# A decoder layer in float32: the low part of every fourth gate/up weight unit made by an accumulating DMA in place of VectorE

## The reference

```
def swiglu(h, w_gate, w_up, w_down):
    return (jax.nn.silu(h @ w_gate) * (h @ w_up)) @ w_down
...
        h = rms_norm(x, norm_ffn[layer])
        x = x + swiglu(h, w_gate[layer], w_up[layer], w_down[layer])
    return rms_norm(x, norm_final)
```

## Time and profile before

| | |
|---|---|
| median of 3 runs | 1426.72 us (1426.65 to 1428.62) |
| span of the profiled execution, from first to last instruction | 1425.4 us |
| time of the profiled execution beside its span | none is given apart from it; the median of the runs is 1.3 us longer than the span |
| TensorE busy | 1413.8 us, 99% |
| DVE busy | 785.1 us, 55% |
| ACT busy | 650.4 us, 46% |
| POOL busy | 42.6 us, 3% |
| DMA, all queues | 260.10 MB, mean 182 GB/s |

### The profile page before, as it was taken

The page is one execution under the profiler, slowest core; times in us unless marked ns, Lnnn a source line. Parts: engine busy times, 40 slices in busy tenths (PEclk is TensorE's granted clock), DMA queues, the critical chain, the costliest instruction groups (busy, mean ns, idle before and its releaser), DMA issues.

```text
span 1425.4 us, 17803 instructions
## 1 busy us (share of the span) xinstructions
PE 1413.8 (99%) x6433; PEld 1155.3 (81%) x6433; DVE 785.1 (55%) x944; ACT 650.4 (46%) x810; POOL 42.6 (3%) x62
## 2 busy tenths in 40 slices
PE   9999999999999999999999999999999999999997
PEld 8999887777788888888888888888888878888886
DVE  6455567667655658655555454554555554544354
ACT  7433356656545654454543333434343333434343
POOL 4000000000000110000000000000000000000000
PEclk9999999999999999999999999999999999999999
DMA  7766665454565666555666666666666666555563
GB/s 243 202 188 187 195 216 168 133 147 135 150 190 162 190 200 210 177 179 182 183 184 181 188 181 186 178 188 185 184 179 188 183 197 196 187 192 188 172 206 118
DMA packets 138272, 260.10 MB, mean 182 GB/s; under 512 B 8448, under 2 KB 29504, under 8 KB 137840
## 3 DMA queue, kind: packets, MB, share of 16 engines
q1 hardware_dynamic: 137552, 256.08, 60.5%
q0 software_dynamic: 640, 3.37, 0.7%
q10 hardware_dynamic: 32, 0.01, 0.0%
HBM read 257.33 MB, written 2.10 MB: 182 GB/s over the span
## 4 chain that ended last, share of the span: by engine, by line
PE 99%; DMA 0%; ACT 0%; DVE 0%; issue 0%; SPq 0%; ACTq 0%; DVEq 0%
PE bank L566 31%; PE bank L568 31%; PE bank L567 31%; PE bank L553 2%; PE bank L709 1%; PE bank L631 0%; DMA x<-in_x 0%; PE bank L708 0%; PE bank L601 0%; PE bank L603 0%; PE bank L602 0%; PE bank L632 0%; PE bank L756 0%; PE bank L748 0%; PE bank L734 0%; PE bank L762 0%
## 5 line engine op out<-in xcount | busy, mean ns | idle before, releaser
L1096 DVE TENSOR_TENSOR weight_lo_ring<-raw_ring,weight_hi_ring 128x1024 fp32r<-128x1024 f32 (+2 forms) x488 | 594.4, 1221 | 547.9 <-ACT weight_hi_ring L911 375.6
L911 ACT ACTIVATE weight_hi_ring<-raw_ring 128x1024 fp32r<-128x1024 f32 (+1 forms) x284 | 295.6, 1042 | 456.8 <-PE bank L568 455.0
L566 PE MATMUL bank<-weight_hi_ring,hT_hi 128*128 128x512 f32 (+2 forms) x768 | 306.0, 398 | 0.0
L904 ACT ACTIVATE weight_hi_ring<-raw_ring 128x1024 fp32r<-128x1024 f32 (+2 forms) x204 | 213.2, 1050 | 200.9 <-PE bank L568 185.2
L568 PE MATMUL bank<-weight_hi_ring,hT_lo 128*128 128x512 f32 (+2 forms) x768 | 296.3, 386 | 0.0
L567 PE MATMUL bank<-weight_lo_ring,hT_hi 128*128 128x512 f32 (+2 forms) x768 | 296.2, 386 | 0.0
L566 PE MATMUL bank<-weight_hi_ring,h2T_hi 128*128 128x512 f32 x704 | 278.4, 395 | 0.0
L568 PE MATMUL bank<-weight_hi_ring,h2T_lo 128*128 128x512 f32 x704 | 277.5, 394 | 0.0
L567 PE MATMUL bank<-weight_lo_ring,h2T_hi 128*128 128x512 f32 x704 | 277.4, 394 | 0.0
L566 PEld LDWEIGHTS bank<-weight_hi_ring,hT_hi 128*128 128x128 f32 x768 | 144.8, 189 | 29.1 <-issue 3.6
L567 PEld LDWEIGHTS bank<-weight_lo_ring,hT_hi 128*128 128x128 f32 x768 | 144.9, 189 | 27.1 <-issue 2.6
(11 more groups left out here) (200 smaller groups left out, 759.5 us busy)
## 6 DMA issues: line engine op xcount, KB each, us to landing
raw_ring<-in_w_in SPq DMA_DIRECT2D x96, 512.0 KB, 3.6
raw_ring<-in_w_gate SPq DMA_DIRECT2D x88, 512.0 KB, 4.3
raw_ring<-in_w_up SPq DMA_DIRECT2D x88, 512.0 KB, 3.8
raw_ring<-in_w_down SPq DMA_DIRECT2D x88, 512.0 KB, 4.4
raw_ring<-in_w_in SPq DMA_DIRECT2D x56, 452.0 KB, 3.5
raw_ring<-in_w_out SPq DMA_DIRECT2D x32, 512.0 KB, 3.8
raw_ring<-in_w_br_c SPq DMA_DIRECT2D x16, 256.0 KB, 4.6
raw_ring<-in_w_br_a SPq DMA_DIRECT2D x16, 256.0 KB, 7.5
```

The costliest lines, as they stand in the source:

```text
L566: pe.matmul(dst, x_hi, w_hi, start=first and k == 0, stop=False)
L904: act.activation(whi[:, s, :, 0:width(u)], raw[:, s, :, 0:width(u)], ACT.Copy).then_inc(hi_ready, 1)
L911: act.activation(whi[:, s, :, 0:cols], raw[:, s, :, 0:cols], ACT.Copy).then_inc(hi_ready, 1)
L1096: dve.tensor_tensor(lo, w, hi.bitcast(F32), ALU.subtract).then_inc(lo_ready, 1)
```

## The change

In the hardware loop of gate and up (ten iterations), the units of slot 3, every fourth, get their low part in another way: ACT writes `-raw`, rounded to float32r, into `wlo` right after the high part, and a DMA issued by POOL adds `raw` onto it. That is 4 units an iteration, 40 in all (`A_UNITS`). DVE leaves them out. The DMA counts in `lo_added`, for which TensorE waits ahead of these units. Since the DMA reads `raw`, SP may load over slot 3 only when it is through; SP waits for `unit_used` of the unit there in place of `lo_ready`, in all 11 iterations and for the first units of slot 3 in the down stage. As DVE no longer counts every unit, `lo_ready` becomes four semaphores, one a slot.

```
+A_FIRST = U_FFN + 2 * UPC + LAG
+A_UNITS = (NC_F - 1) * 2 * UPC // RING
+
+
+def made(u):
+
+    return u // RING + 1 - (A_UNITS if u % RING == RING - 1 and u >= U_DOWN else 0)
...
-        lo_ready = sem("lo_ready")
+        lo_ready = [sem(f"lo_ready{i}") for i in range(RING)]
+        negated = sem("hi_negated")
+        lo_added = sem("lo_added_by_dma")
...
                     for j in range(UPC):
                         u0 = U_FFN + c * UPC + j
-                        sp.wait_ge(lo_ready, i * (2 * UPC) + (u0 - RING + 1))
+                        if u0 % RING == RING - 1:
+                            sp.wait_ge(unit_used, i * (2 * UPC) + (u0 - RING + 1))
+                        else:
+                            sp.wait_ge(lo_ready[u0 % RING], i * (2 * UPC // RING) + made(u0 - RING))
                         load(u0 % RING, w[:, UK * j:UK * j + UK, bass.ts(i, W)])
...
                         u0 = U_DOWN + c * UPD + j
-                        sp.wait_ge(lo_ready, i * (2 * UPD) + (u0 - RING + 1))
+                        if (c, j) == (0, RING - 1):
+                            sp.wait_ge(unit_used, i * (2 * UPD) + (u0 - RING + 1))
+                        else:
+                            sp.wait_ge(lo_ready[u0 % RING], i * (2 * UPD // RING) + made(u0 - RING))
...
+            for n in range(A_UNITS):
+                pool.wait_ge(negated, n + 1)
+                pool.dma_start(wlo[:, RING - 1, :, :], raw[:, RING - 1, :, :],
+                               accum_op=ALU.add).then_inc(lo_added, 16)
+
             pool.wait_ge(unit_used, U_DOWN)
...
                         u0 = U_FFN + c * UPC + j
-                        pe.wait_ge(lo_ready, i * (2 * UPC) + (u0 + 1))
+                        if u0 % RING == RING - 1:
+                            pe.wait_ge(lo_added, i * 64 + (16 * ((c * UPC + j) // RING + 1) - 64))
+                        else:
+                            pe.wait_ge(lo_ready[u0 % RING], i * (2 * UPC // RING) + made(u0))
...
                 for j in range(2 * UPC):
                     split_in_loop(U_FFN + LAG + j, i * (2 * UPC // RING), i * (2 * UPC))
+                    if j % RING == 0:
+                        act.activation(wlo[:, RING - 1, :, :], raw[:, RING - 1, :, :], ACT.Copy,
+                                       scale=-1.0).then_inc(negated, 1)
...
                     u0 = U_FFN + LAG + j
-                    split_unit(u0 % RING, i * (2 * UPC) + (u0 + 1))
+                    if j % RING != 0:
+                        split_unit(u0 % RING, i * (2 * UPC) + (u0 + 1))
```

More of the change, by code:

```diff
@@ L385, in load, with free @@
                 sp.dma_start(raw[:, slot, :, :], src).then_inc(raw_ready[slot], 16)
-            def free(count):
-                sp.wait_ge(lo_ready, count)
+            def free(v):
+                sp.wait_ge(lo_ready[v % RING], made(v))
             def straight(u):
@@ L393, in straight @@
                 if u >= RING:
-                    free(u - RING + 1)
+                    free(u - RING)
                 if kind == "mlp":
@@ L573, in unit @@
             def unit(u, lhs, q, j, n, width=W):
-                pe.wait_ge(lo_ready, u + 1)
+                pe.wait_ge(lo_ready[u % RING], made(u))
                 m = products(u % RING, lhs, q % 2, j == 0, j == n - 1, UK * j, width,
@@ L878, in _ @@
                         u0 = U_DOWN + c * UPD + j
-                        pe.wait_ge(lo_ready, i * (2 * UPD) + (u0 + 1))
+                        pe.wait_ge(lo_ready[u0 % RING], i * (2 * UPD // RING) + made(u0))
                         products(u0 % RING, (actT_hi, actT_lo), q % 2, j == 0, False, UK * j).then_inc(unit_used, 1)
@@ L1095, in split_unit @@
                 lo, w, hi = (m[:, slot, :, 0:cols] for m in (wlo, raw, whi))
-                dve.tensor_tensor(lo, w, hi.bitcast(F32), ALU.subtract).then_inc(lo_ready, 1)
+                dve.tensor_tensor(lo, w, hi.bitcast(F32), ALU.subtract).then_inc(lo_ready[slot], 1)
             def split(u):
```

## The result

The changed kernel takes 1576.7 us in the median of 4 runs (1572.97 to 1578.26), the kernel before 1426.68: a ratio of 1.1044, with 95% interval [1.1031, 1.1058], or 150 us more. The forecast was 1634 us, in a range of 1500 to 1830, and slower.

What follows compares the result with a forecast made beforehand. TensorE was taken to bound the kernel. Forty rounds growing 4.6 us gave 184 us, less 9 for transposes, plus 32 for clock: 207 us onto 1426.7, about 1634 us, range 1500 to 1830.

Steps and rivals of the forecast that it cites:

- The bound: Whole kernel: TensorE is busy 99% of the span, so taking work from DVE gains 0 us.
- The chain of a slot 3 round: Gate/up loop: load 4.2, ACT's passes 2.0, hand-overs 0.3, X, unit 2.8; round 9.3 + X instead of 11.2 us.
- the late load: Slot 3's load starts 8.7 us later; with DVE still making the low part, 6.7 us fits under 8.4, costing 0 us.
- X: Time from POOL's issue of the adding DMA to its landing in the gate/up loop, chosen as 6.5 us.
- prediction's own formula: Gate/up loop: 40 rounds each grow by X - 1.9 us, less 9 for transposes, plus 32 for clock.
- 1 MB row: `norm_final`'s 7.1 us transfer on POOL's queue, beside loads, taken as nearest to 512 KB read twice.
- lower bound of 3.4 us: POOL's queue: 64 KB took 3.4 us and 4 KB 3.5, so X is hardly under 3.4.
- The clock: Behind slot 3 stalls: clock falls about 3.0 us into idle time, costing 0.8 us a round, 32 us; ends 0 and 64.
- The cheap transfer: Adding DMA: X from 3.4 to 4.5 us, stalls too short for the clock, 1478 to 1522 us; chance 0.12.
- the expensive one: Adding DMA slower than twice a copy: X over 10, up to 13.3 us, time up to 1938 us; chance 0.14.
- The hidden one: Adding DMA lands within 1.9 us, chain fits in 8.4 us, TensorE never waits, 1427 us; chance 0.02.
- settle at its lower level: Loop clock stays low: a unit takes 5.6 us, a round 22.4, total 1875 us; chance 0.04.

Runs made afterwards that it cites:

- version with both waits early: Changed kernel with SP's slot 3 load waiting for the adding DMA instead of unit_used, and ACT's negation ahead of the high part: 1427.91 us, ratio 1.0002.
- plain copy: Changed kernel with POOL's DMA copying `raw` onto `wlo` instead of adding it: 1485.33 us, ratio 1.0405.
- half-size DMA: Changed kernel with the adding DMA over only the first of two blocks, 256 KB: 1496.82 us, ratio 1.0477.
- the fillers: Changed kernel with 11 unneeded matmuls ahead of TensorE's wait for the adding DMA, 40 times: 1542.22 us, ratio 1.0798.

## Why the prediction was right

**The bound.** TensorE bounds the kernel and DVE has slack: right. The version with both waits early leaves DVE out in the same 40 units and is neither faster nor slower.

**The chain of a slot 3 round.** Right in each link. Without the DMA the late load costs nothing (forecast 0 us), and what is taken from a link comes back 40 times, with some clock on top: 1.0 us of ACT gave 41 us, 2.1 us of transfer 91 (26 of them clock), and a load one unit earlier 144, since the chain then nearly fits in the round.

**The sizes.** The term that was off is X, chosen as 6.5 us and measured as 5.1 (4.5 to 6.2 in the loop). With 5.1 in the prediction's own formula the round grows by 5.1 - 1.9 = 3.2 us: 40 x 3.2 - 9 + 32 = 151 us, against 150. That it meets so closely is luck in part: the load took 3.7 us in the mean of the 40 rounds and not 4.2, as it stands ahead of its bunch, while the unit took 4.0 with the clock's loss in it and not 3.6, since the first matmul behind a stall takes 0.50 us, and ACT's part with the hand-overs 2.4 and not 2.3. These errors cancel. With X smaller and the load sooner the stalls were 1.5 to 3.8 us, 106 in all, where 4 to 5 and about 180 were forecast.

X was too high because I took it from the 1 MB row of 7.1 us; that the weight loads beside it had lengthened that row is likely, and no run shows it. What sets the 5.1 is in the traces. I took, for each adding DMA, how long after POOL's issue the last load of the bunch landed. In the six kernels with the whole transfer there are 240. Where the last load was in within 2.1 us, 104 of 105 took 4.5 to 4.8 us. The other 135 landed 2.3 to 2.8 us after that last load (mean 2.4), however long it took, up to 6.3 us from issue. The plain copy and the half-size DMA landed 1.2 to 1.3 us after a load as late as that. So here the transfer came through when the loads issued ahead of it had, and the second read shows again as twice the time. It is a relation over the traces of eight kernels; no run took the loads away. In the changed kernel 31 of the 40 were of the late kind, with the fillers 11: that is the 5.1 against 4.5. The plain copies met a bunch further along (its last load landed 1.7 us after POOL's issue in the median, 2.7 in the changed kernel), which is the other 1.0 of their 2.1 us.

The lower bound of 3.4 us, from small transfers at the kernel's start, was no bound: the plain copy of 512 KB landed in 3.0.

By the fit of the Trainium skill ("DMA: Bandwidth & Descriptors", Anatomy of one DMA) the plain copy takes an estimated 3.2 us; this case's trace agrees, with 3.0. The rule of the Trainium skill that an add needs two source reads ("Collectives: The Full Stack", The bandwidth ceiling) would, with that fit, make the adding one an estimated 4.4; the runs show 4.5 at the least and 5.1 in the median, and engine time of 2.7 us against 1.4 for the copy, which agrees with the two reads. The 1470 and 1518 us that the prediction gave by these two have no clock in them; with its 32 us they are 1502 and 1550, still short of 1577.

**The clock.** I took half of the 64 us, by choice and not by a row, and reckoned with a fall about 3.0 us into an idle time. The size was right, 33 us for 32, and that was luck too: of the 40 windows of 4 us behind a stall, 20 have a clock under 0.70 and 20 one of 1.00 (the first, one between and the last of them):

```profile
724.75:728.75 4.00, 4.00 (x9) 3.14 (x10) 0.00 (x0) 0.00 (x0) 0.00 (x0) 0.50 0.00 0
...
864.19:868.19 4.00, 4.00 (x17) 3.28 (x18) 0.40 (x1) 0.82 (x2) 0.00 (x0) 1.00 0.00 0
...
1315.96:1319.96 4.00, 4.00 (x12) 3.22 (x13) 0.75 (x1) 0.00 (x0) 0.00 (x0) 0.66 0.00 0
```

The lower clock did fall on the unit behind the stall; but it fell in other stalls than reckoned, as the last section shows.

**The rivals.** The cheap transfer (X under 4.5) and the expensive one (over 10) fell by X itself. The hidden one fell in this kernel, though it is what the version with both waits early does, and not by a landing within 1.9 us: the chain was shortened at its other end. The clock did not settle at its lower level. What stays open is why the bunch of loads ends later in the changed kernel, 8.6 us after its first issue in the mean, and 8.2 with the fillers. It was not tried.

## What to carry to other kernels

Before a piece of work is moved from an engine with slack to a DMA, add up the ring's chain from "slot free" to "data ready" and set it against the time that the other slots give. Here an estimated 6.7 us of 8.4 became 11.2, and the DMA itself was less than half of that. Count in what stands in the DMA queues when it starts: here the landing followed the last load of the bunch. And ask what the new reader does to the wait that frees the buffer: waiting for the nearest event that makes the slot safe (the DMA landed), and not for a later one that implies it (the unit used), was worth 144 of 150 us. A stall on TensorE costs more than its length when the clock falls behind it, here 4.7 us in the median for a unit that takes 3.1 behind a stall at the full clock.

## What the hardware showed that I had not expected

The clock can fall after TensorE has taken up its work again. Windows of 1 us around one stall of the changed kernel (TensorE idle until 848.34, for 3.56 us; the number before the DMA share is the granted clock):

```profile
848.00:849.00 1.00, 0.66 (x3) 0.58 (x4) 0.25 (x1) 0.00 (x0) 0.00 (x0) 1.00 0.00 0
849.00:850.00 1.00, 1.00 (x5) 0.80 (x4) 0.00 (x0) 0.00 (x0) 0.00 (x0) 0.80 0.00 0
850.00:851.00 1.00, 1.00 (x4) 0.79 (x3) 0.00 (x0) 0.00 (x0) 0.00 (x0) 0.50 0.00 0
...
852.00:853.00 1.00, 1.00 (x3) 0.73 (x3) 0.00 (x0) 0.00 (x0) 0.00 (x0) 0.50 0.00 0
853.00:854.00 1.00, 1.00 (x6) 0.80 (x5) 0.00 (x0) 0.00 (x0) 0.00 (x0) 0.99 0.11 10
```

It was granted in full through the idle time, fell to its lower level at about 849.6, 1.3 us after the first matmul, and came back at about 853.0. Nor did a stall's length alone decide it: none of the ten stalls under 2.0 us had the low clock behind it, but of the longer ones one of 2.27 us (ahead of 907.73) had it and one of 3.54 us (ahead of 953.83) had not.
